# Experts as plain fp32 products on two column tiles, scatter on two row tiles, and fifteen weight slots

## The reference, cut to what matters

```python
y = sum over e of gw[:, e] * ((silu(h @ gate[e]) * (h @ up[e])) @ down[e])
out = x + y
```

## Time and profile before

| | |
|---|---|
| median of three runs | 2022.34 us |
| the profiled execution | 2024.56 us |
| its span, first to last instruction | 2022.5 us |
| share of the span busy | TensorE 95%, VectorE 70%, ScalarE 58%, GpSimd 4% |
| weights and other data read from HBM | 428.61 MB |
| granted TensorE clock, mean | 0.988 |

### The profile page before, as it was taken

One profiled execution on the slowest core, in us unless ns is written; L12 is line 12 of the kernel. 1 busy time (PEld: TensorE's weight loads), 2 busy tenths in 40 slices (PEclk: granted clock), 3 DMA queues, 4 the chain that ended last, 5 costly groups with the idle time before them and its releaser, 6 DMA issues.

```text
span 2022.5 us, 29372 instructions
## 1 busy us (share of the span) xinstructions
PE 1928.6 (95%) x12498; PEld 1723.4 (85%) x12498; DVE 1409.1 (70%) x1397; ACT 1165.6 (58%) x1304; POOL 72.9 (4%) x90
## 2 busy tenths in 40 slices
PE   7999999999999998999999999999889999999997
PEld 6989998978998998998988999887778888888875
DVE  4876558546555776638646555747689999999996
ACT  4643345544444643335555444464398888888884
POOL 0000022000000000013000000000000000000000
PEclk9999999999999998999999999999899999999999
DMA  7433374545453444366535555322469999999994
GB/s 294 155 136 139 138 260 163 187 146 188 173 187 131 177 162 146 105 228 218 200 125 176 188 187 192 136 97 112 155 262 372 377 376 376 376 378 376 378 391 155
DMA packets 64520, 440.80 MB, mean 218 GB/s; under 512 B 7372, under 2 KB 7372, under 8 KB 14592
## 3 DMA queue, kind: packets, MB, share of 16 engines
q1 hardware_dynamic: 55296, 399.63, 52.9%
q0 software_dynamic: 8096, 35.30, 4.7%
q10 hardware_dynamic: 992, 3.93, 0.5%
HBM read 428.61 MB, written 10.23 MB: 217 GB/s over the span
## 4 chain that ended last, share of the span: by engine, by line
PE 64%; DVE 23%; ACT 8%; POOL 1%; issue 1%; DMA 1%; DVEq 0%; ACTq 0%; POOLq 0%
PE psum L191 63%; DVE ring_low L205 7%; ACT hl L201 3%; DVE arena L215 3%; DVE ht L205 3%; DVE rounded L205 2%; DVE hl L205 2%; DVE rounded L215 2%; DVE arena L205 2%; POOL arena L205 1%; ACT arena L201 1%; PE psum L195 1%; DVE resid L205 1%; ACT rounded L201 1%; ACT L201 1%
## 5 line engine op out<-in xcount | busy, mean ns | idle before, releaser
L205 DVE TENSOR_TENSOR hl<-ring,hl 128x2048 fp32r<-128x2048 f32 (+1 forms) x190 | 433.3, 2286 | 310.4 <-ACT hl L201 310.0
L191 PE MATMUL psum<-ht,hl 128*128 128x256 f32 x4992 | 623.0, 286 | 7.4 <-DVE ht L205 6.0
L191 PEld LDWEIGHTS psum<-ht,hl 128*128 128x128 f32 x4992 | 608.3, 193 | 18.2 <-DVE ht L205 7.3
L201 ACT ACTIVATE hl<-ring 128x2048 fp32r<-128x2048 f32 (+1 forms) x286 | 536.0, 1896 | 115.5 <-PE psum L191 105.5
L191 PE MATMUL psum<-hl,ax 128*128 128x512 f32 x1320 | 346.3, 392 | 2.0 <-ACT gn L201 1.3
L201 ACT ACTIVATE arena<-psum 128x512 f32<-128x512 f32 (+4 forms) x226 | 119.2, 527 | 389.1 <-PE psum L191 351.1
L191 PEld LDWEIGHTS psum<-hl,ax 128*128 128x128 f32 x1320 | 246.7, 188 | 53.9 <-ACT gn L201 1.7
L205 DVE TENSOR_TENSOR ring_low<-ring,hl 128x2048 fp32r<-128x2048 f32 x96 | 215.3, 2285 | 20.6 <-ACT hl L201 20.4
L191 PE MATMUL psum<-arena 128*128 128x128 f32 (+8 forms) x1520 | 168.2, 290 | 6.7 <-DVE arena L205 4.4
L191 PEld LDWEIGHTS psum<-arena 128*128 128x128 f32 (+3 forms) x1520 | 153.3, 177 | 18.2 <-DVE arena L205 4.7
L191 PE MATMUL psum<-rounded 128*128 128x512 f32 (+2 forms) x640 | 132.4, 335 | 5.8 <-DVE par L205 3.1
(11 more groups left out here) (122 smaller groups left out, 1994.3 us busy)
## 6 DMA issues: line engine op xcount, KB each, us to landing
ring<-W SPq DMA_DIRECT2D x284, 1024.0 KB, 5.1
arena<-W SPq DMA_DIRECT2D x48, 1024.0 KB, 8.0
ht_raw<-W SPq DMA_DIRECT2D x46, 1024.0 KB, 7.6
gate_d<-arena POOLq DMA_DIRECT2D x32, 256.0 KB, 3.8
arena<-gate_d POOLq DMA_DIRECT2D x8, 1024.0 KB, 8.1
gn<-GB POOLq DMA_DIRECT2D x10, 512.0 KB, 4.2
arena<-GB POOLq DMA_DIRECT2D x6, 512.0 KB, 5.2
ring<-W SPq DMA_DIRECT2D x4, 512.0 KB, 5.7
```

The lines of the kernel that those rows point to most:

```text
L191: return Nothing() if self.e is None else self.e.matmul(o, a, b, start=start, stop=stop, skip_group_check=skip_group_check)
L201: return self.e.activation(o, a, f, bias=bias, scale=scale)
L205: return Nothing() if self.e is None else self.e.tensor_tensor(o, a, b, op)
```

## The change

It concerns the experts and the loads of their weights.
- **Plain products.** The experts' weights are no longer cut into parts: `whole(u)` is true for them, and TensorE waits for the DMA itself. The gathered tokens are plain fp32 with 64 columns (`XE`). `gate_up(e, c)` now takes half c of the depth for gate and up together: gate's products go to PSUM partitions 0 to 63, up's to 64 to 127 of the same bank, in turn. `down` does the same with its two column halves. The results are 64 tokens at one time in each half of the partitions.
- **Silu and product before the turn.** ScalarE takes silu of gate from PSUM, VectorE multiplies by up (64 x 512), TensorE transposes the product (4 transposes), VectorE copies it out (`aT`). `gu`, `fold` and the splits of `aT` and `YE` are gone.
- **Scatter** is 4 plain products, two on rows 0 to 63 and two on rows 64 to 127 of the array, in turn. `SE` is plain fp32.
- **Order on TensorE**: gate_up(e+1, 0), turn_(e), place(e+1), scatter(e-1), gather, gate_up(e+1, 1), down(e).
- **Fifteen slots**: the ring's 4, `ht_raw` 2, the memory of the parts (`hl_raw`) 6, the arena 3. The first fifteen expert units are loaded ahead of the flag, each as its memory falls free; behind the flag each waits for the unit that had its slot. Four slots of the ring serve all units before.
- **After the norm** only the plain tokens (`hf`, half by ScalarE, half by VectorE) and `XS` are written; the split of `ht` and the cuts of m0 and m1 are gone.
- The way `many` gets plain products too; it isn't taken here.

```diff
-                def gate_up(e, q):
+                def gate_up(e, c):
                     g, i = divmod(e, 4)
...
+                    two = [weights() for _ in range(2)]
+                    pe.wait_ge(s_act, A["x", g, 2 * c + 1])
+                    for k in range(4):
+                        for s, (_, w) in enumerate(two):
+                            ins = pe.matmul(psum[64 * s:64 * s + 64, into(e), :], mo.XE[g % 2][:, 4 * c + k, 64 * i:64 * i + 64],
+                                            w[:, k, :], c == 0 and k == 0, c == 1 and k == 3)
+                    ins.then_inc(s_pe, P("gu", e, c))
...
+                def turn_(e):
+                    pe.wait_ge(s_dve, V["hid", e])
+                    for k in range(4):
+                        ins = pe.transpose(psum[:, shared, 64 * k:64 * k + 64], mo.hid[:, 128 * k:128 * k + 128],
+                                           C("ident")[64:128, 64:128])
...
+                    for k in range(4):
+                        for j, (_, w) in enumerate(two):
+                            ins = pe.matmul(psum[64 * j:64 * j + 64, shared, :], mo.aT[:, k, :], w[:, k, :], k == 0, k == 3)
...
                     for t in range(2):
                         for j in range(2):
+                            js = slice(64 * j, 64 * j + 64)
+                            ins = pe.matmul(psum[:, 2 * t + j, :], mo.SE[e % 3][js, t, :], mo.YE[e % 2][js, :], e == 0, e == 31)
...
                     if e:
-                        pe.wait_ge(s_dve, V["YE", e - 1])
+                        pe.wait_ge(s_act, A["YE", e - 1])
...
                 n, had = slot_at[u], slot_had[u]
+                m = u - u_moe
+                if had is not None and whole(had):
                     sp.wait_ge(s_pe, P["unit", had])
                 elif had is not None:
                     sp.wait_ge(s_dve, V["lo", had])
+                elif m == 0:
+                    sp.wait_ge(s_pe, P["xg"])
+                elif 6 <= m < 12:
+                    sp.wait_ge(s_pe, P["unit", u_moe - 3 + (m - 6) // 2])
+                elif m == 12:
+                    sp.wait_ge(s_pe, P["b2 end"])
+                    sp.wait_ge(s_act, A["ynorm", 0])
+                    sp.wait_ge(s_dve, V["b2 end"])
+                elif m == 14:
+                    sp.wait_ge(s_pe, P["n2", 1, 1])
+                    sp.wait_ge(s_dve, V["xl"])
```

More of the change, by code:

```diff
@@ L22 @@
 LOOK = 2
-MORE = 2
+SLOTS = 15
 KEYS = 2
@@ L1225, in tensor, with weights @@
             mm(psum[:, b, 64:96], [(C("ones"), mo.mk[:, 0, :]), (C("ones"), mo.mk[:, 1, :])]).then_inc(s_pe, P("counts"))
+            def weights():
+                u = now["unit"]
+                now["unit"] = u + 1
+                pe.wait_ge(s_w[slot_at[u]], landed[u])
+                return u, raw(u)
             def few():
@@ L1229, in few, with into @@
                     bank("few", n, keep=True)
-                into, beside = 4, 6
-                acc = {(t, j): 2 * t + j for t in range(2) for j in range(2)}
+                shared, placed = 6, 7
+                def into(e):
+                    return 4 + e % 2
                 def gather(g, i, b):
@@ L1257, in place @@
                     ins.then_inc(s_pe, P("place", e))
-                def gate_up(e, q):
+                def gate_up(e, c):
                     g, i = divmod(e, 4)
[L1261 to L1268, removed]
+                    two = [weights() for _ in range(2)]
[5 more added lines that the diff above has]
+                    ins.then_inc(s_pe, P("gu", e, c))
+                    for u, _ in two:
@@ L1338, in expert_in @@
                 def expert_in(e):
-                    for nm in ("dg", "du"):
-                        two = [unit() for _ in range(2)]
+                    four = [weights() for _ in range(4)]
+                    for n, nm in enumerate(("dg", "du")):
                         for i in (0, 2):
@@ L1889, in scalar @@
             for t in range(2):
-                norm_cut(hTv, t, "n2")
-            unit()
-            ac.wait_ge(s_dve, V["n2", "xn", 1, 1])
-            copy(mo.XS[0], mo.n2.xn, "xh")
+                ac.wait_ge(s_pe, P["n2", t, 1])
+                act(mo.hf[:, 4:8, 128 * t:128 * t + 128], heads4(banks["n2", t, 1]), ACT.Copy, "hf", t, after=False)
+                gone("n2", t, 1)
+            act(mo.XS[0], mo.n2.xn, ACT.Copy, "xh", after=False)
             ac.wait_ge(s_pe, P["logits"])
@@ L1907, in few @@
             def few():
-                into, beside = 4, 6
-                def cut(n):
-                    for _ in range(n):
-                        if now["split"] < n_units:
-                            upper()
-                def pair(b):
-                    return flat(psum[:, b:b + 2, :])
+                shared, placed = 6, 7
                 def gather(g, i, b):
                     ac.wait_ge(s_pe, P["gather", g, i])
-                    act(flat(mo.XE[g % 2][i // 2][:, 2 * (i % 2):2 * (i % 2) + 2, :]), pair(b), ACT.Copy, "x", g, i, after=False)
+                    act(flat(mo.XE[g % 2][:, 2 * i:2 * i + 2, :]), psum[:, b, :], ACT.Copy, "x", g, i, after=False)
@@ L1928, in gate_up, with gate @@
+                def gate(e):
                     ac.wait_ge(s_pe, P["gu", e, 1])
-                    act(mo.gu, pair(into), ACT.Copy, "gu", e, after=False)
-                def turn_(e):
-                    ac.wait_ge(s_pe, P["turn", e])
-                    if e:
-                        ac.wait_ge(s_dve, V["hid", e - 1])
-                    act(mo.sg, half(beside, 0), ACT.Silu, "sg", e, after=False)
+                    act(mo.sg, psum[0:64, 4 + e % 2, :], ACT.Silu, "sg", e, after=False)
@@ L1937, in down @@
                 def down(e):
                     ac.wait_ge(s_pe, P["ye", e])
-                    if e:
-                        ac.wait_ge(s_pe, P["scatter", e - 1])
                     ac.wait_ge(s_act, A["gs", e])
-                    act(mo.YE[0], pair(beside), ACT.Copy, "YE", e, scale=mo.gs[:, e:e + 1], after=False)
+                    act(mo.YE[e % 2], psum[:, shared, :], ACT.Copy, "YE", e, scale=mo.gs[:, e:e + 1], after=False)
                 for i in range(4):
-                    gather(0, i, beside if i % 2 else into)
+                    gather(0, i, shared if i % 2 else 5)
@@ L1961, in few @@
                     if g < 8:
-                        gather(g, i, beside)
-                    if e < 31:
-                        gate_up(e + 1)
-                    cut(2)
+                        gather(g, i, shared)
                 down(31)
@@ L1972, in many @@
             def many():
-                sg = mo.dsg
-                def expert_in(e):
+                for e in range(32):
                     for i in (0, 2):
-                        unit()
                         ac.wait_ge(s_pe, P["dg", e, i])
@@ L2656, in vector @@
             for t in range(2):
-                for j in range(2):
-                    ve.wait_ge(s_act, A["n2", "hi", t, j])
-                    copy(mo.hf[:, 4 * j:4 * j + 4, 128 * t:128 * t + 128], heads4(banks["n2", t, j]), "hf", t)
-            for t in range(2):
-                norm_cut(hTv, t, "n2")
-            unit()
+                ve.wait_ge(s_pe, P["n2", t, 0])
+                copy(mo.hf[:, 0:4, 128 * t:128 * t + 128], heads4(banks["n2", t, 0]), "hf", t)
+                gone("n2", t, 0)
             ve.wait_ge(s_act, A["xh"])
@@ L2705, in few @@
             def few():
-                into, beside = 4, 6
-                def cut(n):
-                    for _ in range(n):
-                        if now["split"] < n_units:
-                            lower_part()
+                shared = 6
                 def prep(g):
```

241 lines of the change are left out of this document (87 added, 154 removed).

## The result

The changed kernel takes **1931.36 us**, median of four runs (1928.21 to 1932.25), against 2022.64 before: a ratio of 0.9536, 95% interval 0.9517 to 0.9554. The profiled execution takes 1932.25 us, its span is 1930.5. The forecast of 1948 had the direction and the mechanism; the time fell by 91 us where 74.6 were forecast, and lies 2.6 us under the range of 1934 to 1988.

The account below looks back on a forecast made before the run. The prediction saw a 16.66 us loop over VectorE, TensorE and ScalarE, with DMA nearly full. Start 1465.3 + 32 x 14.8, less 3.8, plus 2 x 0.8, put TensorE's end at 1937, the time at 1948; range 1934 to 1988.

Parts of the forecast that it names:

- Pairs of tiles at full rate: Experts' products on TensorE: two tiles run fully side by side, 0.432 us a slot of 512 columns.
- The price of no pairing: Rival, gate_up, down and scatter: 28 slots become 56, +12.1 us an expert, +387 us, 2335; chance 0.05.
- the rival at 2032: Gate_up and down: stationary-operand loads can't run under products in flight, 2.6 us an expert, 84 us; chance 0.05.
- The start: First gate_up at about 1465.3 instead of 1471.15: router's logits 4.3 us earlier, then 4.4 instead of 5.8 us.
- The covers: Silu, product and copies run during TensorE's products, priced at nothing; only YE(30) and YE(31) uncovered, 2 x 0.8 us.
- Two limits close together: End of the experts: last weights land at 1926, down(31) wants them at 1931, 5 us apart; holds down to 403 GB/s.
- 14.8 us an expert: TensorE's work per expert in the new loop, 1.86 us less than the old 16.66.
- a change of form: TensorE entering or leaving tiled form: 0.1 to 0.2 us, 0.15 taken, five per expert, 0.75 us.
- stays: After TensorE's last product: adding and storing the output take as long as before.
- The DMA's own limit as far as this trace shows it: Weight loads: 408 GB/s, read from the old kernel's last 40 us; 2.57 us a unit, 15.4 us an expert.
- DMA as the bound at 376: Rival, weight loads: engines stay at 376 GB/s whatever the queue, 36 us later, 1984; chance 0.15.
- Uncovered waits: Rival, expert loop: an uncovered chain, gate_up to silu to product to turn, 2 us an expert, 2012; chance 0.05.

Follow-up runs that it names:

- e3: Changed kernel with all gate_up and down products but the last of each group sent to the same 64 array columns: 2207 us.
- e1: Changed kernel with scatter(e-1) moved ahead of place(e+1), three changes of tiled form per expert instead of five: 1932.2 us, ratio 0.956.
- e5: Changed kernel with six weight slots, one expert's weights, instead of fifteen: 1978.3 us, of which 8 us are a late start.
- e2: Changed kernel with gate_up and down products of one column tile first, then those of the other, instead of in turn: 2000 us.
- e12: Changed kernel with scatter(e-1) ahead of place(e+1), and down units from m15 on loading only half their bytes: 1924.1 us.

## Why the prediction was right or wrong

**Right, with the size it gave:**
- Pairs of tiles at full rate: 0.432 us a slot forecast, 0.43 measured. The price of no pairing was right too: e3 takes 20 pairs apart and costs 22.96 - 14.39 = 8.57 us, 0.43 each.
- Loads of the stationary operand cost nothing that can be seen between these products, and the rival at 2032 fell: sixteen loads and sixteen products in two column tiles take 3.44 us, eight slots of 0.43, twice the 0.216 of 256 columns. In one tile (e3) sixteen of each take 6.96, 0.435 a pair of load and product, so nothing is seen of the loads there either.
- The start: 1465.3 forecast, 1464.64 measured, and its parts, 4.3 us from the shorter work of VectorE (4.8, of which 0.7 came from ahead of the norm: the products of 1440.42 start at 1439.68) and 1.4 from the gathers (1.7). That the sum fits within 0.7 us is in part luck: e1, with the same program up to there, starts its first gate_up at 1460.54, because the part ahead ran 5 us earlier in that execution (those products start at 1434.65).
- The covers: no wait for silu, product or copies, except the two that were named at the end, 0.78 and 0.79 us.
- Two limits close together. But TensorE was to be the later by 5 us; in the trace the loads were, by two waits of 1.15 us in sum, and the experiments found the two limits within about 2 us.

**Wrong: the size of three terms, all on the same side.** The step that failed is "14.8 us an expert"; it is 14.39. The list of works in it was good: 13.85 without changes of form, against 14.39 - 5 x 0.12 = 13.79 (e1's 0.12, seen between row tiles and the whole array, taken for all five: an estimate). But a change of form was put at 0.15 where e1 shows at most 0.12, 0.15 us was added for semaphores where nothing is to be seen, and 13.85 + 0.75 = 14.60 was written as 14.65: with the 0.06 by which the works were too high, 0.41 us in all. Times 32 this is 13.1 of the 14.0 us by which the last scatter came early: its fourth instruction ends at 1922.67, and 1938.9 - 3.8 + 1.6 gives 1936.7 ("1937"). Each extra was small, and all stood on the safe side. That the old loop lost 0.5 us an expert to its waits was no evidence for the new one, in which nothing waits for another engine.

From the chain of waits of the changed kernel, the last scatter:

```profile
1921.52 1.15 PE psum L190 x4
```

A small term was put at "stays": what follows the last product. From the same reading to the end of the profiled time it was 2024.56 - 2012.86 = 11.7 us before and is 1932.25 - 1922.67 = 9.6 now. Some 2 us of that lie between the landing of the output and the end of the span (2.8 us before, 0.8 after); no run shows why. The works of the experts alone would have left 1948 - 13.1 = 1934.9, just inside the range; these 2.1 us, and 1.4 of smaller ones such as the start, put the time outside.

The other large term hid behind the first. "The DMA's own limit as far as this trace shows it", 408 GB/s, is 421. At 408 the last landing would have come 177 x 0.08 = 14 us later, at 1929 instead of 1915.3, TensorE's end 8.2 us behind it as here, at 1937.5, and the profiled time would have been near 1946 (8.7 more), inside the range. And 408 was no limit. In the 40 us from which it was read the old kernel's chain of waits is VectorE's, one expert in 15.79 us:

```profile
1954.35 1.20 DVE rounded L215
...
1970.14 1.20 DVE rounded L215
```

6.29 MB in 15.79 us is 398 GB/s, and no engine waited for a landing there: the DMA engines followed the loop, as they did at 376, and their share of 1.00 did not say that they could give no more. In e5, where each unit also waits for its slot, the rate is 404 at a share of 0.99; in every run with nine or more slots and whole units it is 421, but for the two that TensorE alone slows (e2, e3). The range's lower end took small values for TensorE's work and for the start, and left the rest at its middle, with some us for an unforeseen wait: it should have asked what all low values give together with a faster DMA.

**The rivals:** DMA as the bound at 376 did not come, though at 421 the DMA engines became one of two limits. Uncovered waits did not come.

## What to carry to other kernels

Where a loop is full on several engines at once, count what each would need alone after the change, and price the next limit as carefully as the first: here 91 us came from one edit, and then an edit that is worth 6.6 us where the loads have room (e12) gave nothing, because the loads ended the stage where they did before. Put work for two tiles of the array in turn in the program: here the same products in two blocks cost 69 us more (e2). A transfer rate at a full share of the DMA engines need not be their limit (408 GB/s at 1.00 before, 421 at 1.01 after): ask whether anything waited for it. Take the range's ends from all low values together, not from one.

## What was not expected of the hardware

- In pairs of column tiles, 16 instructions of a plain fp32 product, 512 columns each, took 3.44 us (changed kernel, down, 1611.42 to 1614.86), 0.215 each. One of the single-instruction kind on all columns took 0.228 before (96 from 1417.67 to 1439.55). The 8 `matmul` calls of one gate_up or down stand in the changed kernel's trace as 16 instructions, two a plain product (x16 at 1607.94 and at 1611.42). Before, a group of 8 blocks of weights had 16 calls, one for the upper and one for the lower part of each, and 16 instructions (x16 at 1471.15).
- Loads from HBM ran at 421 GB/s from 1480 to 1910 in the changed kernel, 430 us on end, at a share of 1.01, with TensorE busy 429.31 of the 430 us and its 512-column products starting two by two, 10 ns apart (1598.32 and 1598.33). With six slots (e5) it was 404 from 1500 to 1900, at a share of 0.99.
- A change between row tiles and the whole array cost at most 0.12 us: e1 has two fewer an expert, and its period is 14.16 us against 14.39.
- With the tiles' products in two blocks (e2), the second block's work started (1604.10) ahead of three of the first's eight (1604.52 the first of them) and reached into the next group: 16.38 us an expert, against 14.39 in turn (changed kernel) and 22.96 in one tile (e3).
